# Gates of a decoder step projected feature by token from tokens scaled in place, instead of projected by token and turned

## The chip, the cores and the metric

One Trainium2 chip, one core of it. The metric is the device time of one execution in microseconds (us). All data are 32-bit floats. The engines are called by their names in the profile: PE (TensorE matmul), PEld (its weight load), DVE (VectorE), ACT (ScalarE), POOL (GpSimd) and SP (SyncE, which here only starts transfers).

## The reference, cut to what matters

The step serves 512 prompt tokens and 8 sampled ones. Each token is normed, projected by one wide matrix, attended in two head groups, gated with SiLU and projected back:

```python
def project(x, pos, lp):
    h = rms_norm(x, lp['norm_w'])
    q_n, kv_c, kv_s, kv_w, g_n, z_n, q_d, k_d, v_d, z_d = split_proj(h @ lp['w_in'])
    ...

def layer_output(x, o_branches, g_n, z_n, o_d, z_d, lam_init, lp):
    o_nsa = jnp.sum(o_branches * g_n[..., None], axis=2).reshape(B, T, NSA_WIDTH)
    o_d = (rms_norm(o_d, lp['diff_out_norm']) * (1.0 - lam_init)).reshape(B, T, DIFF_WIDTH)
    o = jnp.concatenate([o_nsa * jax.nn.silu(z_n), o_d * jax.nn.silu(z_d)], axis=-1)
    return x + o @ lp['w_out']
```

`rms_norm` multiplies a token by its inverse root mean square and by a weight for each feature. `z_n` and `z_d` are the gates: 512 features each, for every token.

## The kernel before

**Projection.** The 1024x4096 projection is cut into 8 chunks of 512 columns (one of them 280 wide) and 4 tiles of 128 tokens, so tile `n` of 32 is chunk `n // 4`, tokens `128 * (n % 4)` onward. `xt` holds the tokens turned (feature on the partitions, 8 blocks `k`), already multiplied by the feature weights but not by the inverse root means. A tile is 8 matmuls (two records each in the profile) with tokens stationary and 512 columns of weights moving (`tile`, L652); the result lies token by feature in one of two banks. ACT's `keep_tile` copies it to `proj` and multiplies by the token's inverse root mean `x_rs` (one number for each partition) on the way (L1212). For tiles 20 to 27, the gates, it also writes `exp(-z)` to `z_tmp` (L1218) and DVE's `silu_z` makes `z / (1 + exp(-z))` of the two (L1696 to L1698). The 8 sampled tokens have their own matmuls in `new_projection` (L611), scaled later by DVE's `sum_new`.

**Turning.** What comes later wants most parts feature by token. PE's `turn_blocks` transposes four 128x128 blocks into a bank (L691) and ACT's `keep_turn` copies the bank back over its source (L1258). There are 28 such turns; the last eight, `z0` to `z7`, are the gates: 32 transposes and 8 copies.

**Order.** Every engine runs one list written out by hand; semaphores join them. On PE: tiles 0 to 3; then a stage over 8 cached sequences `b` with `first_layer(b)` (L630), `second_layer(b)` (L641), two tiles each, and score matmuls of the paged cache (`k_step`, L666) between them; then 16 steps `i`, each with `tile(16 + i)` and small work. The steps at the end are:

- `i == 12`: tile 28, then 32 small score matmuls (L862), which DVE masks and centres (L1794 to L1800).
- `i == 13`: tile 29, then `z0` to `z3`.
- `i == 14`: tile 30, transposes of the window probabilities (L873) and of the compressed probabilities (L878, after DVE's `c_probs`, set at L1826), then `z4`, `z5`, then 32 matmuls that turn and weigh the differential probabilities (L888, after DVE's `diff_weights`, set at L1842, and ACT's copies of L878's result, L1359).
- `i == 15`: tile 31, one small matmul (L894), then `z6`, `z7`.

After these comes the prompt attention, 64 duos `j`: PE `scores_of` (L934), DVE `mask_max` (L1862, L1863), ACT `exps` (L1382), DVE `scale`, PE `turn` (L952), with cached value steps (L905) between. Before its first `mask_max` DVE reads L894's result (L1844) and makes the gates of the sampled tokens (L1848 to L1851).

**Early part on DVE.** `a_hidden(b)` (L1589 onward) follows each `first_layer(b)`; `a_hidden(1)` and `sum_new(1)` (L1562, L1564) stand just ahead of `a_hidden(2)`.

**Transfers.** SP loads weight chunks, cache pages and, once tile 31 is done, the cached values. A chunk of weights or a set of pages is asked for when PE has finished with the buffer's last content.

Of the kernel before, what the change touches and what calls it, by code (L numbers as in the profile page):

```python
# [7 lines left out]
ALU = mybir.AluOpType  # L8
# [3 lines left out]
P = 128  # L12
# [159 lines left out]
def program(nc, src, dst):  # L172
    ctx = ExitStack()
    with ctx:
# [99 lines left out]
        win_v = xn[:, :].rearrange("p (b k n) -> p b k n", b=DEC, k=4)  # L274
        new_z_exp = sample[:, 0:2048].rearrange("p (u n) -> p u n", u=2)[:, :, 0:512]
        row_max, row_sum = att[:, 0:8].rearrange("p (s c) -> p s c", c=2), att[:, 8:16].rearrange("p (s c) -> p s c", c=2)
        c_max, neg_rs, eps_col, out_norm = att[:, 16:48], att[:, 48:52], att[:, 52:53], norm_w[:, KC:KC + 1]
        p_turned_n = xn[:, :].rearrange("p (c k n) -> p c k n", c=4, k=TILES)
        c_exp = proj[:, :, C_KVC:C_KVC + 256].rearrange("p t (g n) -> p g t n", g=2)

# [49 lines left out]
        def bc(ap, n, at):  # L330
# [11 lines left out]
        V_NONE, V_MORE = (2, 32, 37, 40, 44, 58), (13, 16, 54, 61)  # L342

        TURNS = ["qd0", "qd1", "qd2", "qd3", "kc0", "kc1", "kc2", "kc3", "kd0", "kd1", "kv0", "kv1", "kd2", "kd3",
                 "qn0", "qn1", "qn2", "qn3", "ks", "kw", "z0", "z1", "z2", "z3", "z4", "z5", "z6", "z7"]
        N_TURNS = len(TURNS)

        def turn_number(name):
# [1 line left out]

        def turn_home(name):
            at = {"qd": C_QD, "kd": C_KD, "qn": C_QN, "kv": C_KVC, "ks": C_KS, "kw": C_KW}
            col = C_ZN + P * int(name[1:]) if name[0] == "z" else at[name[:2]] + (P * int(name[2:]) if len(name) > 2 else 0)
            return proj[:, :, col:col + P]

        def width(c):

# [232 lines left out]
        def _(pe):  # L590
# [54 lines left out]
            def tile(n):  # L645

                c, t = n // TILES, n % TILES
                if t == 0:
                    pe.wait_ge(s(w_turn(c)[0]), w_turn(c)[1])
                pe.wait_ge(s("proj_kept"), n - 1)  # L650
                for k in range(KC):
                    last = mm(banks[:, 3 + n % 2, 0:width(c)], xt[:, k, P * t:P * t + P], w_ring[:, c % 2, k, 0:width(c)],  # L652
                              start=k == 0, stop=k == KC - 1)
                last.then_inc(s("proj_ready"), 1)

            def k_step(n):
# [56 lines left out]
            new_projection(1)  # L713
            tile(5)
            second_layer(1)
            for b in range(2, DEC):
                at = K_TURN * (b - 2)
                first_layer(b)
                for n in range(at, at + 2):
                    k_step(n)  # L720
                if b < DEC - 1:
                    if b in (3, 5):
                        new_projection(b // 2 + 1)
                    tile(2 * b + 2)
                    for n in range(at + 2, at + 4):
                        k_step(n)
                    second_layer(b)
                    tile(2 * b + 3)
                else:
                    for n in range(at + 2, at + 4):  # L730
                        k_step(n)
                    pe.wait_ge(s("new_normed"), 2)
                    pe.wait_ge(s("new_proj_used"), 4)
                    cols = [C_QN + P * r for r in range(GRP)] + [C_KD + P * j for j in range(4)] + [C_KS, C_KW]
                    for n, c in enumerate(cols):
                        last = tr(banks[:, 5, 8 * n:8 * n + 8], sample[:, c:c + P], ident[0:DEC, 0:DEC])
                    last.then_inc(s("new_turned"), 1)
                for n in range(at + 4, at + k_turns(b)):
                    k_step(n)


            for i in range(16):
# [114 lines left out]
                if i == 12:  # L857
# [5 lines left out]
                                          proj[64 * g:64 * g + 64, t, C_QN + P * r:C_QN + P * r + P], p_kc_t[64 * g:64 * g + 64, :],  # L863
                                          start=True, stop=True, tile_position=(64 * g, 0))
                    last.then_inc(s("c_scored"), 1)
                if i == 13:
                    pe.wait_ge(s("z_done"), TILES)
                    for k in range(4):
                        turn_blocks(f"z{k}")
                if i == 14:  # L870
                    pe.wait_ge(s("win_vector"), step("win_probs"))
                    for kt in range(4):
                        last = tr(banks[:, 2, 64 * kt:64 * kt + 64], p_win[:, P * kt:P * kt + P], ident[0:64, 0:64])  # L873
                    last.then_inc(s("win_tensor"), 1)
                    pe.wait_ge(s("c_probs"), 1)
                    for g in range(2):
                        for t in range(TILES):
                            last = tr(banks[:, 6 + g, P * t:P * t + P], c_exp[:, g, t, :], ident)  # L878
                    last.then_inc(s("c_turned"), 1)
                    pe.wait_ge(s("z_done"), 2 * TILES)  # L880
                    turn_blocks("z4")
                    turn_blocks("z5")
                    pe.wait_ge(s("diff_weights"), 1)
                    pe.wait_ge(s("c_turned_kept"), 2)
                    for g in range(PAGES):
                        if g % 8 == 0 and g >= 16:
                            pe.wait_ge(s("probs_kept"), g // 8 - 1)
                        last = mm(banks[:, 6 + (g // 8) % 2, 64 * (g % 8):64 * (g % 8) + 64], scores[:, P * g:P * g + P], d_weights,  # L888
                                  start=True, stop=True)
                        if g % 8 == 7:  # L890
                            last.then_inc(s("probs_turned"), 1)
                if i == 15:
                    pe.wait_ge(s("new_proj_used"), 8)
                    mm(banks[0:DEC, 5, 0:DH], own_rows, own_weights, start=True, stop=True).then_inc(s("own_weighted"), 1)  # L894
                    turn_blocks("z6")
                    turn_blocks("z7")

            def v_step(v):

# [294 lines left out]
        def _(act):  # L1194
# [10 lines left out]
            def keep_tile(n):  # L1205

                c, t = n // TILES, n % TILES
                act.wait_ge(s("proj_ready"), n + 1)
                if n == 12:
                    act.wait_ge(s("normed"), 2)  # L1210
                of = banks[:, FIRST_BANKS[t] if c == 0 else 3 + n % 2, 0:width(c)]
                last = A(proj[:, t, c * CHUNK:c * CHUNK + width(c)], of, ACT.Copy, scale=x_rs[:, t:t + 1])  # L1212
                if 20 <= n < 28:
                    if n == 20:
                        act.wait_ge(s("head_means"), 4)
                    if n >= 22:
                        act.wait_ge(s("z_done"), n - 21)
                    last = A(z_tmp[:, n % 2, :], of, ACT.Exp, scale=neg_rs[:, t:t + 1])  # L1218
                last.then_inc(s("proj_kept"), 1)

            def sigmoids(b):
# [75 lines left out]
            for i in range(16):  # L1297
# [47 lines left out]
                if i == 12:  # L1345
# [4 lines left out]
                    A(scores, scores, ACT.Exp, bias=work[:, 144:145], accum_out=work[:, 145:146]).then_inc(s("diff_exps"), 1)  # L1350
                    act.wait_ge(s("c_centred"), 1)
                    A(c_exp, banks[:, 6:8, :].rearrange("p g (t n) -> p g t n", t=TILES), ACT.Exp).then_inc(s("c_exps"), 1)
                if i == 13:
                    for k in range(4):
                        keep_turn(f"z{k}")
                if i == 14:
                    act.wait_ge(s("c_turned"), 1)
                    for g in range(2):
                        A(proj[:, :, C_KVC + P * g:C_KVC + P * g + P], banks[:, 6 + g, :].rearrange("p (t n) -> p t n", t=TILES),  # L1359
                          ACT.Copy).then_inc(s("c_turned_kept"), 1)  # L1360
                    keep_turn("z4")
                    keep_turn("z5")
                    for h in range(4):
                        act.wait_ge(s("probs_turned"), h + 1)
                        A(probs_t[:, 8 * h:8 * h + 8, :].rearrange("p g n -> p (g n)"), banks[:, 6 + h % 2, :], ACT.Copy).then_inc(s("probs_kept"), 1)
                    act.wait_ge(s("new_proj_used"), 7)
                    A(new_gates, new_gates, ACT.Exp, scale=-1.0)
                    A(new_z_exp, sample[:, C_ZN:C_ZN + 1024].rearrange("p (u n) -> p u n", u=2), ACT.Exp, scale=-1.0).then_inc(s("new_z_exps"), 1)
                if i == 15:
                    keep_turn("z6")  # L1370
                    keep_turn("z7")
            act.wait_ge(s("proj_ready"), 32)
            act.wait_ge(s("new_proj_ready"), NCHUNK)

# [90 lines left out]
        def _(dve):  # L1465
# [82 lines left out]
            V.tensor_scalar(x_rs[:, :], x_rs[:, :], 1.0 / D_MODEL, EPS, ALU.mult, ALU.add).then_inc(s("x_means"), 1)  # L1548
            dve.wait_ge(s("x_roots"), 1)
            L(V.reciprocal(x_rs[:, :], x_rs[:, :]))  # L1550
            V.tensor_scalar(neg_rs, x_rs[:, 0:TILES], -1.0, None, ALU.mult).then_inc(s("x_rs_ready"), 1)

            dve.wait_ge(s("w1_in"), 48)
            L(V.tensor_tensor(pos_w1.rearrange("p k h l e -> p (k h l) e"), w1.rearrange("p k h l e -> p (k h l) e"),
# [61 lines left out]
            last.then_inc(s("q_placed"), 1)  # L1616
            a_hidden(1)
            sum_new(1)
            a_hidden(2)
            means_of(0, early_tmp)  # L1620
            a_hidden(3)
# [68 lines left out]

            def silu_z(n):

                c, t = n // TILES, n % TILES
                e, z = z_tmp[:, n % 2, :], proj[:, t, c * CHUNK:(c + 1) * CHUNK]
                dve.wait_ge(s("proj_kept"), n + 1)
                L(V.tensor_scalar(e, e, 1.0, None, ALU.add))  # L1696
                L(V.reciprocal(e, e))  # L1697
                V.tensor_tensor(z, z, e, ALU.mult).then_inc(s("z_done"), 1)  # L1698

            dve.wait_ge(s("cmp_tensor"), step("cmp_scored"))  # L1700
            V.tensor_reduce(small[0:64, 62:63], banks[0:64, 2, 0:NCMP], AX.X, ALU.max, negate=True).then_inc(s("cmp_vector"), 1)
# [464 lines left out]
```

## Time and profile before

| what | us |
|---|---|
| median of 3 executions | 790.75 |
| lowest, highest | 786.97, 792.52 |
| the profiled execution, first to last instruction | 792.1 |
| PE busy in it | 735.8 |
| DVE busy in it | 438.4 |
| ACT busy in it | 206.8 |

PE is busy in 93% of the span and leads the chain of work that ended last. Its busy time includes matmuls that overlap, so it tells how full the engine's list is and not how near the array is to its limit. Times below are microseconds from the first instruction of the profiled execution.

### The profile page before, as it was taken

How to read it: one execution, taken by the hardware profiler on the slowest of the kernel's cores; microseconds unless marked ns; L12 is line 12 of the kernel's file. 1: busy time of each engine (PE TensorE's matmuls, PEld its weight loads, DVE VectorE, ACT ScalarE, POOL GpSimd, SP SyncE). 2: the span in 40 equal slices, each digit the busy share in tenths (PEclk: the TensorE clock that was granted, in tenths of full speed). 3: DMA queues.
4: the chain of work that ended last, by engine and by line, in shares of the span. 5: the costliest groups of instructions: out<-in, count | busy, mean ns of one | idle time of the engine just before them, and what ended most of it. 6: DMA issues, size and time to landing. Idle time of an engine off the chain costs nothing.

```text
span 792.1 us, 14734 instructions
## 1 busy us (share of the span) xinstructions
PE 735.8 (93%) x4779; PEld 356.7 (45%) x4779; DVE 438.4 (55%) x945; ACT 206.8 (26%) x524; POOL 82.9 (10%) x155
## 2 busy tenths in 40 slices
PE   7999999999999999998999996898897887999997
PEld 3465645453545456443544562334443452433542
DVE  3351250805704357997563838957768656645273
ACT  0411011102010213122233323534455334333200
POOL 0000000000000000020002016500746200000000
PEclk9999999999999999998999997999999976999999
DMA  8997987999898989979788129988899939984621
GB/s 327 306 319 214 339 279 253 298 353 351 296 371 282 378 314 365 373 262 390 254 282 279 37 92 305 334 304 275 250 317 318 296 131 387 364 280 142 262 112 55
DMA packets 134552, 220.72 MB, mean 279 GB/s; under 512 B 17642, under 2 KB 58771, under 8 KB 133259
## 3 DMA queue, kind: packets, MB, share of 16 engines
q1 hardware_dynamic: 113754, 194.75, 71.7%
q0 software_dynamic: 6080, 13.25, 5.0%
q10 hardware_dynamic: 14640, 11.77, 4.8%
q8 instruction: 38, 0.62, 0.3%
q14 instruction: 40, 0.32, 0.1%
HBM read 213.84 MB, written 10.04 MB: 283 GB/s over the span
## 4 chain that ended last, share of the span: by engine, by line
PE 57%; DVE 17%; SPq 10%; DMA 8%; issue 4%; ACT 2%; POOL 0%; ACTq 0%; DVEq 0%
PE banks L652 13%; PE banks L630 13%; SPq L428 8%; PE banks L905 4%; PE banks L1036 4%; PE banks L666 4%; DMA proj<-in_cmp_cache 3%; PE banks L1157 3%; DVE att L1863 3%; DMA ring<-in_dv_cache 3%; PE banks L934 2%; PE banks L976 2%; PE banks L952 2%; DVE banks L1862 1%; PE banks L969 1%
## 5 line engine op out<-in xcount | busy, mean ns | idle before, releaser
L652 PE MATMUL banks<-ring,xt 128*128 128x512 f32 (+1 forms) x448 | 188.4, 574 | 0.0
L652 PEld LDWEIGHTS banks<-ring,xt 128*128 128x128 f32 x448 | 83.8, 192 | 93.8 <-issue 91.1
L630 PE MATMUL banks<-proj,wide 128*64 128x256 f32 x896 | 99.9, 384 | 2.2 <-DMA proj<-in_cmp_cache 2.1
L1382 ACT ACTIVATE wide<-banks,att 128x384 f32<-128x384 f32 (+3 forms) x128 | 66.4, 524 | 133.4 <-DVE att L1863 132.2
L630 PEld LDWEIGHTS banks<-proj,wide 128*64 128x64 f32 x896 | 66.3, 139 | 38.2 <-DMA proj<-in_cmp_cache 5.8
L905 PE MATMUL banks<-ring,small 128*32 128x512 f32 x512 | 71.6, 640 | 4.9 <-DMA ring<-in_dv_cache 3.3
L1589 DVE TENSOR_SCALAR small<-small 128x510 f32<-128x510 f32 x8 | 3.4, 427 | 122.8 <-ACT small L1227 106.3
L1212 ACT ACTIVATE proj<-banks,x_rs 128x512 f32<-128x512 f32 (+1 forms) x32 | 21.2, 664 | 177.0 <-PE banks L652 142.1
L666 PE MATMUL banks<-ring,small 128*32 128x512 f32 x512 | 61.4, 598 | 2.1 <-DMA ring<-in_dk_cache 2.0
L934 PE MATMUL banks<-proj 64*128 64x384 f32 (+7 forms) x256 | 54.7, 505 | 6.9 <-ACT wide L1382 6.9
L446 POOL DMA_DIRECT2D ring<-in_sel_cache x104 | 55.4, 533 | 32.9 <-issue 28.9
L1862 DVE TENSOR_TENSOR banks<-banks,consts 128x256 f32<-128x256 f32 x64 | 27.4, 428 | 55.6 <-PE banks L934 55.1
L1863 DVE TENSOR_REDUCE att<-banks 128x2 f32<-128x768 f32 (+3 forms) x64 | 52.8, 825 | 2.2
L952 PE MATMUL banks<-consts,wide 128*128 128x128 f32 x240 | 41.9, 297 | 11.9 <-DVE xt L1887 4.8
L952 PEld LDWEIGHTS banks<-consts,wide 128*128 128x128 f32 x240 | 27.7, 148 | 44.1 <-issue 18.0
L934 PEld LDWEIGHTS banks<-proj 32*128 32x128 f32 (+1 forms) x256 | 20.4, 195 | 53.6 <-issue 39.4
L598 PE MATMUL banks<-ring,xt 128*128 128x512 f32 x64 | 30.3, 638 | 5.8 <-DVE xt L1545 5.8
L1227 ACT ACTIVATE small<-banks,bias 128x255 f32<-128x255 f32 x16 | 6.7, 470 | 101.4 <-PE banks L630 88.0
L666 PEld LDWEIGHTS banks<-ring,small 128*32 128x32 f32 x512 | 13.4, 109 | 41.8 <-issue 34.9
L1157 PE MATMUL banks<-ring,proj 128*128 128x512 f32 x64 | 30.5, 630 | 0.0
L1036 PE MATMUL banks<-ring,proj 128*128 128x512 f32 x64 | 30.4, 610 | 0.0
L1697 DVE RECIPROCAL small<-small 128x512 f32<-128x512 f32 x8 | 26.8, 3353 | 0.3
(360 smaller groups left out, 829.9 us busy)
## 6 DMA issues: line engine op xcount, KB each, us to landing
ring<-in_dk_cache SPq DMA_DIRECT2D x256, 256.0 KB, 5.7
ring<-in_dv_cache SPq DMA_DIRECT2D x256, 256.0 KB, 5.5
proj<-in_cmp_cache SPq DMA_DIRECT2D x144, 128.0 KB, 3.9
ring<-in_w_in SPq DMA_DIRECT2D x6, 2048.0 KB, 12.1
proj<-in_cmp_cache ACTq DMA_DIRECT2D x80, 128.0 KB, 5.4
ring<-in_x_nat SPq DMA_DIRECT2D x2, 2048.0 KB
ring<-in_cmp_cache SPq DMA_DIRECT2D x32, 128.0 KB, 4.2
ring<-in_w_out SPq DMA_DIRECT2D x2, 2048.0 KB, 11.9
```

The costliest lines, as they stand in the source:

```text
L428: eng.dma_start(to(g), rows).then_inc(done, 16)
L446: eng.dma_start(sel_kv[64 * (n % 2):64 * (n % 2) + 64, q % 8, n // 2, :], src["sel_cache"][bass.ds(at, 1), :, :].rearrange("o k n -> (o k) ...
L630: last = mm(to, w1[:, kv, half, lp, :], rows[:, kv, g, lp, :, :, :], start=lp + half == 0, stop=lp == LP - 1 and half == 1, tile_position= ...
L652: last = mm(banks[:, 3 + n % 2, 0:width(c)], xt[:, k, P * t:P * t + P], w_ring[:, c % 2, k, 0:width(c)], start=k == 0, stop=k == KC - 1)
L666: last = mm(banks[32 * j:32 * j + 32, 6 + i % 2, :], q_blk[:, j, b, :], k_ring[:, n % 4, :, P * j:P * j + P], start=b == 0, stop=b == DEC - 1,
L905: last = mm(banks[32 * i:32 * i + 32, 7, :], probs_t[:, 4 * st + i, 32 * (b // 4):32 * (b // 4) + 32], k_ring[:, st % 4, i, :], start=st = ...
L934: last = mm(banks[:, 2 * (j % 2) + c, 0:n].rearrange("p (k n) -> p k n", n=P), proj[at:at + rows, t, q:q + P], proj[at:at + rows, 0:t + 1, ...
L952: last = tr(banks[:, 4 + (kind if kind < 2 else c), P * k:P * k + P], e_slot(j, c)[:, P * k:P * k + P], ident)
L1036: last = mm(banks[:, 6, :], out_block(t, k), w_out[:, k, 512 * c:512 * c + 512], start=k == 0, stop=k == KC - 1)
L1157: last = mm(banks[:, 2 * t + c, :], out_block(t, k), w_out[:, k, 512 * c:512 * c + 512], start=k == 0, stop=k == KC - 1)
L1382: last = A(e_slot(j, c)[:, 0:n], banks[:, 2 * (j % 2) + c, 0:n], ACT.Exp, bias=row_max[:, j % 4, c:c + 1], accum_out=row_sum[:, j % 4, c:c ...
L1863: V.tensor_reduce(row_max[:, j % 4, :], both[:, :, 0:n], AX.X, ALU.max, negate=True).then_inc(s("maxed"), 1)
```

## The change

Two sets of edits belong together. First, the prompt tokens in `xt` are multiplied by their inverse root means. For this PE spreads `x_rs` over the partitions (four matmuls of 128x128, with a column of `x_rs` broadcast as the stationary side and the identity moving, into bank 7), placed after `second_layer(1)`; DVE then multiplies `xt` in place by that bank, placed after `sum_new(1)`. DVE waits for tiles up to 5 (they still use the unscaled tokens), and tile 6 waits for DVE. From tile 6 on ACT copies with a scale of 1.

Second, the gate tiles 20 to 27 exchange the operands: a block of 128 weight columns is stationary and all 512 tokens move, so that a tile is 128 features by 512 tokens and goes straight to its place in `z_t`. The turns `z0` to `z7` and their copies go, and with them two waits of PE for `z_done`.

```diff
         TURNS = ["qd0", "qd1", "qd2", "qd3", "kc0", "kc1", "kc2", "kc3", "kd0", "kd1", "kv0", "kv1", "kd2", "kd3",
-                 "qn0", "qn1", "qn2", "qn3", "ks", "kw", "z0", "z1", "z2", "z3", "z4", "z5", "z6", "z7"]
+                 "qn0", "qn1", "qn2", "qn3", "ks", "kw"]
...
+        Z_TILES = range(20, 28)
+        X_NORMED = 6
+
+        def tile_home(n):
+
+            c, t = n // TILES, n % TILES
+            if n in Z_TILES:
+                return z_t(n - Z_TILES[0])
+            return proj[:, t, c * CHUNK:c * CHUNK + width(c)]
...
                 pe.wait_ge(s("proj_kept"), n - 1)
+                if n == X_NORMED:
+                    pe.wait_ge(s("x_normed"), 1)
                 for k in range(KC):
-                    last = mm(banks[:, 3 + n % 2, 0:width(c)], xt[:, k, P * t:P * t + P], w_ring[:, c % 2, k, 0:width(c)],
-                              start=k == 0, stop=k == KC - 1)
+                    if n in Z_TILES:
+                        of, by = w_ring[:, c % 2, k, P * t:P * t + P], xt[:, k, 0:SEQ]
+                    else:
+                        of, by = xt[:, k, P * t:P * t + P], w_ring[:, c % 2, k, 0:width(c)]
+                    last = mm(banks[:, 3 + n % 2, 0:width(c)], of, by, start=k == 0, stop=k == KC - 1)
...
             tile(5)
             second_layer(1)
+            for t in range(TILES):
+                last = mm(banks[:, 7, P * t:P * t + P], x_rs[:, t:t + 1].broadcast_to([P, P]), ident, start=True, stop=True)
+            last.then_inc(s("rs_spread"), 1)
...
-                if i == 13:
-                    pe.wait_ge(s("z_done"), TILES)
-                    for k in range(4):
-                        turn_blocks(f"z{k}")
...
-                    pe.wait_ge(s("z_done"), 2 * TILES)
-                    turn_blocks("z4")
-                    turn_blocks("z5")
                     pe.wait_ge(s("diff_weights"), 1)
                     pe.wait_ge(s("c_turned_kept"), 2)
...
-                    turn_blocks("z6")
-                    turn_blocks("z7")
...
-                last = A(proj[:, t, c * CHUNK:c * CHUNK + width(c)], of, ACT.Copy, scale=x_rs[:, t:t + 1])
-                if 20 <= n < 28:
+                to = tile_home(n)
+                if n in Z_TILES:
+                    of = of.rearrange("p (t n) -> p t n", t=TILES)
+                last = A(to, of, ACT.Copy, scale=x_rs[:, t:t + 1] if n < X_NORMED else 1.0)
+                if n in Z_TILES:
...
-                    last = A(z_tmp[:, n % 2, :], of, ACT.Exp, scale=neg_rs[:, t:t + 1])
+                    last = A(z_tmp[:, n % 2, :].rearrange("p (t n) -> p t n", t=TILES), of, ACT.Exp, scale=-1.0)
...
             a_hidden(1)
             sum_new(1)
+            dve.wait_ge(s("rs_spread"), 1)
+            dve.wait_ge(s("proj_ready"), X_NORMED)
+            x_prompt = xt[:, :, 0:SEQ]
+            V.tensor_tensor(x_prompt, x_prompt, bc(banks[:, 7, :], KC, 1), ALU.mult).then_inc(s("x_normed"), 1)
             a_hidden(2)
```

## Rows read from the trace of the kernel before

**Rows 1.** The page's head: span and instructions.

```profile
span 792.1 us, 14734 instructions
```

**Rows 2.** The chain that ended last, as shares of the span by engine.

```profile
PE 57%; DVE 17%; SPq 10%; DMA 8%; issue 4%; ACT 2%; POOL 0%; ACTq 0%; DVEq 0%
```

**Rows 3.** Windows: stretch, length, busy of each engine (records), granted clock, DMA, GB/s.

```profile
434.00:443.00 9.00, 9.00 (x23) 4.05 (x22) 8.83 (x9) 2.61 (x4) 2.04 (x5) 0.81 0.14 37
...
476.00:484.00 8.00, 2.33 (x14) 0.66 (x12) 7.30 (x13) 1.25 (x5) 5.63 (x11) 0.67 1.04 306
```

**Rows 4.** Timeline of PE, 430 to 483: start, length, line, tiles, records [idle before].

```profile
429.98 3.76 PE L862 MATMUL banks<-picked,proj 64*128 64x32 f32 x64
433.67 8.83 PE L652 MATMUL banks<-ring,xt 128*128 128x512 f32 x16
442.34 1.04 PE L691 MATMUL banks<-consts,proj 128*128 128x128 f32 x8
443.77 1.15 PE L691 MATMUL banks<-consts,proj 128*128 128x128 f32 x8 [0.39 <-ACT proj L1258]
444.75 7.03 PE L652 MATMUL banks<-ring,xt 128*128 128x512 f32 x16
451.71 0.46 PE L873 MATMUL banks<-consts,small 64*128 64x64 f32 x4
452.11 1.09 PE L878 MATMUL banks<-consts,proj 128*128 128x128 f32 x8
...
454.46 7.33 PE L888 MATMUL banks<-work,wide 128*128 128x64 f32 x64 [0.39 <-ACT proj L1359]
461.63 7.08 PE L652 MATMUL banks<-ring,xt 128*128 128x512 f32 x16
...
482.82 1.65 PE L934 MATMUL banks<-proj 64*128 64x384 f32 x4 [5.67 <-ACT wide L1382]
```

**Rows 5.** Timeline of DVE over the same stretch.

```profile
433.79 1.30 DVE L1794 TENSOR_TENSOR banks<-banks,consts 128x512 f32<-128x512 f32 x2 [7.88 <-PE banks L862]
...
450.11 1.29 DVE L1826 TENSOR_TENSOR proj<-proj,att 128x512 f32<-128x512 f32 x2
452.21 0.42 DVE L1830 COPY spread<-banks 128x256 f32<-128x256 f32 x1 [0.81 <-PE banks L873]
...
453.98 0.25 DVE L1842 TENSOR_SCALAR work<-consts,small 128x64 f32<-128x64 f32 x1
468.88 0.15 DVE L1844 COPY small<-banks 8x8 f32<-8x8 f32 x1 [14.66 <-PE banks L894]
...
480.46 0.96 DVE L1863 TENSOR_REDUCE att<-banks 128x2 f32<-128x768 f32 x1
```

**Rows 6.** Timeline of ACT: the copies that L888 waits for.

```profile
453.24 1.08 ACT L1359 ACTIVATE proj<-banks 128x512 f32<-128x512 f32 x2 [0.73 <-PE banks L878]
```

**Rows 7.** Timeline of PE and DVE, 82 to 102.

```profile
82.51 2.31 DVE L1564 SCALAR_TENSOR_TENSOR sample<-banks,x_rs,sample 8x512 f32<-8x512 f32 x3
85.74 1.05 PE L641 MATMUL banks<-w,small 128*128 128x128 f32 x8
86.72 14.03 PE L630 MATMUL banks<-proj,wide 128*64 128x256 f32 x128
...
101.72 0.43 DVE L1589 TENSOR_SCALAR small<-small 128x510 f32<-128x510 f32 x1 [16.90 <-ACT small L1227]
```

**Rows 8.** Groups by line and form: busy, mean ns of one, idle before.

```profile
L1036 PE MATMUL banks<-ring,proj 128*128 128x512 f32 x64 | 30.4, 610 | 0.0
...
L1672 DVE TENSOR_TENSOR xn<-xn,kc_stats 128x2048 f32<-128x2048 f32 x1 | 2.3, 2293 | 0.0
```

**Rows 9.** PE at 122, and windows of PE alone: stretch, length, busy (records), clock, DMA, GB/s.

```profile
122.02 1.06 PE L666 MATMUL banks<-ring,small 128*32 128x512 f32 x8 [1.54 <-DMA ring<-in_dk_cache]
...
124.00:128.00 4.00, 4.00 (x26) 0.61 1.06 389
434.00:438.00 4.00, 4.00 (x6) 0.57 0.17 42
```

More of the change, by code:

```diff
@@ L276, in program @@
         row_max, row_sum = att[:, 0:8].rearrange("p (s c) -> p s c", c=2), att[:, 8:16].rearrange("p (s c) -> p s c", c=2)
-        c_max, neg_rs, eps_col, out_norm = att[:, 16:48], att[:, 48:52], att[:, 52:53], norm_w[:, KC:KC + 1]
+        c_max, eps_col, out_norm = att[:, 16:48], att[:, 52:53], norm_w[:, KC:KC + 1]
         p_turned_n = xn[:, :].rearrange("p (c k n) -> p c k n", c=4, k=TILES)
@@ L352, in turn_home @@
             at = {"qd": C_QD, "kd": C_KD, "qn": C_QN, "kv": C_KVC, "ks": C_KS, "kw": C_KW}
-            col = C_ZN + P * int(name[1:]) if name[0] == "z" else at[name[:2]] + (P * int(name[2:]) if len(name) > 2 else 0)
+            col = at[name[:2]] + (P * int(name[2:]) if len(name) > 2 else 0)
             return proj[:, :, col:col + P]
+        Z_TILES = range(20, 28)
[5 more added lines that the diff above has]
+            return proj[:, t, c * CHUNK:c * CHUNK + width(c)]
         def width(c):
@@ L1352, in _ @@
                     A(c_exp, banks[:, 6:8, :].rearrange("p g (t n) -> p g t n", t=TILES), ACT.Exp).then_inc(s("c_exps"), 1)
-                if i == 13:
-                    for k in range(4):
-                        keep_turn(f"z{k}")
                 if i == 14:
@@ L1360, in _ @@
                           ACT.Copy).then_inc(s("c_turned_kept"), 1)
-                    keep_turn("z4")
-                    keep_turn("z5")
                     for h in range(4):
@@ L1368, in _ @@
                     A(new_z_exp, sample[:, C_ZN:C_ZN + 1024].rearrange("p (u n) -> p u n", u=2), ACT.Exp, scale=-1.0).then_inc(s("new_z_exps"), 1)
-                if i == 15:
-                    keep_turn("z6")
-                    keep_turn("z7")
             act.wait_ge(s("proj_ready"), 32)
@@ L1550, in _ @@
             L(V.reciprocal(x_rs[:, :], x_rs[:, :]))
-            V.tensor_scalar(neg_rs, x_rs[:, 0:TILES], -1.0, None, ALU.mult).then_inc(s("x_rs_ready"), 1)
+            dve.sem_inc(s("x_rs_ready"), 1)
             dve.wait_ge(s("w1_in"), 48)
@@ L1691, in silu_z @@
             def silu_z(n):
-                c, t = n // TILES, n % TILES
-                e, z = z_tmp[:, n % 2, :], proj[:, t, c * CHUNK:(c + 1) * CHUNK]
+                e, z = z_tmp[:, n % 2, :], tile_home(n)
                 dve.wait_ge(s("proj_kept"), n + 1)
@@ L1697, in silu_z @@
                 L(V.reciprocal(e, e))
-                V.tensor_tensor(z, z, e, ALU.mult).then_inc(s("z_done"), 1)
+                V.tensor_tensor(z, z, e.rearrange("p (t n) -> p t n", t=TILES), ALU.mult).then_inc(s("z_done"), 1)
             dve.wait_ge(s("cmp_tensor"), step("cmp_scored"))
```

## Prediction

> **What bounds the kernel now.** I began with the page's head and the chain of work that ended last. The profiled execution spans 792.1 us [rows 1]; the runs' median is 790.75, 0.2% less. I work with differences and add them to the median. PE holds 57% of the chain and DVE 17% [rows 2], so one cannot say for the whole kernel that a microsecond of PE work is a microsecond of time. Each stage has to be read by itself.
>
> The removed work stands at one place, the last three steps before the prompt attention, so next I read the windows there and then the timelines of PE, DVE and ACT side by side. From 434 to 443 PE is full (9.00 of 9.00) but its granted clock is 0.81 on the mean, and DVE is full as well (8.83) [rows 3]. From 476 to 484 PE works 2.33 of 8 us while DVE works 7.30: the attention's first scores lie ready, and DVE still has the sampled tokens' gates to make [rows 3, 5]. PE sits idle 5.67 us there [rows 4]. The reader is to see that two engines take turns at the end of this stage: PE to L862, then DVE and PE side by side, then PE through L888 and tile 31, then DVE alone from 468.88 to the first maxima at 481.4 [rows 4, 5].
>
> **What is removed, and what it is worth.** On PE 32 transposes go, in four pairs of turns. The first two pairs fill the time from tile 29's last matmul (442.34) to tile 30's first (444.75): 2.41 us with a wait of 0.39 for ACT in it [rows 4]. The third pair stands between L878 (which begins at 452.11 and takes 1.09) and L888, about 1 us. The fourth, again about 1 us, stands behind tile 31 and L894. Counted as PE time this is 2.4 + 1.0 + 1.0, some 4.4 us, and with the wait ahead of L888 (0.39) 4.8. I now go through what each is worth on the path.
>
> The first two pairs: without them tile 30 starts at 442.34 and, at 7.03 less the overlap of its start, is through at about 449.4. L873 follows to about 449.8. L878 then waits for DVE's `c_probs`. DVE's list from 433.79 to the end of L1826 at 451.40 has no wait on anything of PE behind L862, and the change takes nothing from it [rows 5]. So L878 starts at about 451.5 and not at 452.11: of 2.4 us, 0.6 us come through, and the rest turns into a wait of PE of some 1.6 us.
>
> The third pair: behind L878 (1.05 us, to 452.55) ACT copies two banks, 1.08 us from 453.24 in the trace, so from 452.6 to 453.7 after the change [rows 6]. L888 waits for this copy before and after; z4 and z5 lay in its shadow. Adding the same 0.13 from ACT's end to PE's start (454.32 to 454.46), L888 begins at 453.8 in place of 454.46. DVE's other release, the end of L1842, was at 454.23 because DVE had waited 0.81 us for L873 [rows 5]; it moves to 453.4 and is not last. The first three pairs together are worth 454.46 - 453.83 = 0.63 us. What was queued behind them on ACT (copies of `probs_turned`) follows L888's matmuls and moves with them.
>
> The fourth pair is off the path. L894 stands before it, DVE takes over at L894's end, and PE's next needed product waits for DVE until 482.82. One microsecond less only makes the idle 5.67 some 1 us longer. The 8 ACT copies lie in ACT's idle time and are worth nothing by themselves. If DVE's list were no longer the cover (the rival below), the whole 4.8 us would count.
>
> **What is added.** (a) The spread: four 128x128 matmuls. These are matmuls and not transposes. The nearest row is `second_layer`: 4 matmuls of the same shape show as 8 records in 1.05 us (0.98 to the next start) [rows 7]. I take +1.0 us. It stands in front of `first_layer(2)`, whose end releases the next page loads, and PE goes on with no gap there. The lower bound is 0.4: SP's loads may absorb part of it, since PE waits for pages (1.54 us at 120.5) soon after [rows 9]. The upper is 1.1.
>
> (b) The scaling in place on DVE, 4096 elements a partition. The nearest row is 2048 elements of two operands in 2.29 us [rows 8], so 4.6 us. It can start when the spread is done, about 87.8. DVE has been idle since 84.8 and has nothing until 101.72, because `a_hidden(2)` waits for `first_layer(2)` [rows 7]. It ends at about 92.5. Tile 6, behind `first_layer(2)` (to 100.7) and two score steps, waits for it but finds it done 9 us before. Cost 0. Were the 14.03 us of `first_layer(2)` not there, the 4.6 would stand open on PE.
>
> (c) The exchanged operands. A gate tile remains 8 matmuls of 128x512 with a 128x128 weight load. The trace has such matmuls with other sources: L1036, ring moving and `proj` stationary, 610 ns a record [rows 8]. In full runs they start about 0.45 us apart against 0.44 (7.03 / 16) in a tile. I take 0; if the gate tiles took that pace, 128 records by 0.013 are +1.7. A gain is excluded, since number, width and weight columns are equal. DVE and ACT keep their elements; the stored pieces only lie apart. No transfer is added or moved, and POOL's list is untouched.
>
> Sum on the path: +1.0 - 0.6 = +0.4 us.
>
> **The clock.** Then there is what the new gap does. PE will have only 0.45 us of L873 and 1.05 us of L878 between 449.4 and 453.8, and then 7.33 us of L888, on which everything waits. The trace shows what follows such stretches. After 1.54 us idle, 1.06 us of narrow matmuls and another 0.42 idle at 120.5 to 123.5, the window from 124 has a granted clock of 0.61, most of it the lower of the two levels, 1.2 GHz in place of 2.4 [rows 9]. After L862's 3.76 us of small matmuls the clock is 0.57 from 434 to 438, and tile 29 takes 8.83 us in place of 7.03 to 7.08: 1.8 us lost [rows 4, 9]. I take it that the clock falls once in the new gap and price it by tile 29's loss, +1.7 us. The bounds are 0 (it does not fall) and about +3 (L878 falls into it too, and the low level goes on into L888). If tile 29 is spared instead, nothing is won: PE only waits longer for DVE.
>
> The Trainium skill speaks against the change here: "TensorE: Matmul & The Clock Gate", section "HAM oscillation — how this bites in real kernels", has TensorE go back to half rate in waits between bursts of matmuls and the next burst start slow. By that rule it would be +2.1 us, without it +0.4. The half-speed stretches above agree; that none follows 451.7 to 454.5 in this trace, where transposes fill the time, speaks neither way.
>
> So +0.4 + 1.7 = +2.1 us, and 790.75 + 2.1 = 792.9.
>
> **Rivals.**
>
> 1. *The clock holds in the gap.* Only the sum counts: 791.2. For it speaks that L878 and L873 break the gap in two. Against it is that the windows above fell after less.
>
> 2. *All the removed PE time comes through.* It needs DVE not to be the bound between 433.8 and 451.4. Then -4.8 + 1.0 = -3.8, so 787.0. Against it stands that DVE is busy with hardly a gap over that stretch.
>
> 3. *Slower.* Weights from the ring as the stationary side and `xt` as the moving one pace the 8 gate tiles worse than any row shows. Each tile lies on PE's path. It decides (over 1% slower, 7.9 us) once a tile takes (7.9 - 2.1) / 8 = 0.7 us more than 7.03. The nearest row gives a fifth of a microsecond, 794.6. At 0.8 us a tile it would be 799.3.
>
> 4. *The scaling is exposed* (its cover is thinner than read): up to 4.6 more, 797.5. It needs DVE to begin 9 us late.
>
> **How the numbers follow.** Forecast 0.50, rival 1 0.32, rival 2 0.06, rival 3 0.08 (of it 0.04 over 1%), rival 4 0.02, the remainder 0.02 anywhere. The runs of before lie from 787.0 to 792.5, so a median is uncertain by about 2 us by itself. The range takes rival 1 with 3 us below (788.0) and the forecast with its upper clock bound and the slower pace (792.9 + 1.3 + 1.7, about 796.0). About 1% is what a measurement of this kernel can tell from no change: faster 0.03, within 1% 0.92, slower 0.05.
>
> **What the profile after would show.** 8 records of a 128x128 matmul ahead of the third `first_layer`, about 1 us. A DVE multiplication of 4.6 us within its idle time and no wait of PE for it. L652 on the gate tiles at 574 to 610 ns. No turn between tiles 29 and 30; a wait of PE on DVE of about 1.6 us ahead of L878, and one on ACT of 1.2 us ahead of L888. A granted clock near 0.5 in a part of L888. An idle of 6 to 7 us before the first scores are used. The prediction is wrong if L878 starts with tile 30's end (DVE had room), if L888 begins less than 19 us after the end of L862 (20.7 before, 20.1 forecast), or if a gate tile takes more than 7.3 us at full clock.

## The result and the profile after

The changed kernel takes 796.61 us on the median of 20 executions (788.39 to 802.77), the kernel before 790.51 (786.2 to 794.97, also 20). The ratio is 1.0068, with a 95% interval of 1.0042 to 1.0093: slower by some 5.4 us, where 2.1 were forecast. It lies within 1%. The ratios here and below leave out executions more than 1.5% above the fastest of the same kernel (here 801.57 and 802.77), so they need not match the medians, which are 6.1 us apart here. The changed kernel's executions fall apart into two groups: three at 788.4, 788.7 and 789.7, and seventeen from 793.9 up.

The page's head and its chain of work, of the changed kernel:

```profile
span 795.9 us, 14679 instructions
...
PE 57%; DVE 19%; SPq 10%; DMA 8%; issue 4%; ACT 2%; POOL 0%; ACTq 0%; DVEq 0%
```

The profiled executions differ by 3.8 us (792.1 before, [rows 1]). As shares the chain has hardly changed [rows 2], so the page doesn't tell where the 3.8 us lie. The timeline of PE around the removed turns does (line numbers of the changed kernel: L880 is the former L862, L887 L873, L892 L878, L899 L888, L668 the tiles):

```profile
425.64 3.76 PE L880 MATMUL banks<-picked,proj 64*128 64x32 f32 x64
429.33 15.70 PE L668 MATMUL banks<-ring,xt 128*128 128x512 f32 x32
444.96 0.46 PE L887 MATMUL banks<-consts,small 64*128 64x64 f32 x4
447.12 1.09 PE L892 MATMUL banks<-consts,proj 128*128 128x128 f32 x8 [1.70 <-DVE proj L1833]
449.47 13.19 PE L899 MATMUL banks<-work,wide 128*128 128x64 f32 x64 [1.27 <-ACT proj L1368]
462.46 9.50 PE L668 MATMUL banks<-ring,xt 128*128 128x512 f32 x16
...
486.06 1.65 PE L943 MATMUL banks<-proj 64*128 64x384 f32 x4 [6.80 <-ACT wide L1386]
```

L899 are the 32 matmuls that turn and weigh the differential probabilities; they are called the weighing matmuls below. Compare with [rows 4]. From the small score matmuls to the weighing matmuls (L862 to L888 before, L880 to L899 after) it is 24.48 us before and 23.83 after: 0.65 less, as forecast. Then the weighing matmuls take 13.19 us where they took 7.33 (+5.9), and tile 31 takes 9.50 where it took 7.08 (+2.4). The windows tell why. Columns as in [rows 3], the granted clock being the last but two:

```profile
445.00:449.00 4.00, 1.51 (x13) 1.13 (x12) 3.66 (x16) 1.35 (x3) 0.00 (x0) 1.00 0.12 33
450.00:462.00 12.00, 12.00 (x59) 12.00 (x59) 0.00 (x0) 1.79 (x3) 0.00 (x0) 0.51 0.13 36
462.00:467.00 5.00, 5.00 (x10) 2.42 (x10) 0.00 (x0) 1.65 (x3) 0.00 (x0) 0.50 0.14 40
467.00:472.00 5.00, 5.00 (x18) 2.00 (x20) 0.00 (x0) 0.01 (x1) 0.00 (x0) 0.97 0.06 17
```

In the gap PE works 1.51 of 4 us. Behind it the granted clock goes to 1.2 GHz, 0.8 us after L899 has begun (at 450.2), and stays there for 17 us, through the rest of L899 and the first half of tile 31. PE is 100% busy in that time; by its busy share nothing is to be seen.

The difference of the two profiled executions, cut at the same marks:

| stretch | before | after | difference |
|---|---|---|---|
| start to the small score matmuls | 430.0 | 425.6 | -4.4 |
| from there to the weighing matmuls | 24.5 | 23.8 | -0.7 |
| weighing matmuls and tile 31, to the small matmul behind (L894, after L905) | 14.2 | 22.4 | +8.2 |
| from there to the first scores behind the wait | 14.2 | 14.2 | 0.0 |
| from there to the first value matmuls (L969, after L978) | 30.6 | 32.5 | +1.9 |
| from there to PE's end | 272.9 | 271.6 | -1.3 |

The first row is no gain of the change; it even holds the added spread. The place where the small score matmuls start moves from profile to profile: 425.6 and 431.1 in two other kernels with the gates turned as before (`before_move31_early` and `scale_only` below). In the profile of before the clock is low at 124 to 128 [rows 9] and again from 366 to 372 (the `new_projection` at 368.15 takes 3.60 us there, 1.90 in the changed kernel's profile), and the waits for cache pages differ by a microsecond or two. Such stretches differ from execution to execution. The +1.9 at the start of the attention is of this sort too: the clock is low for 17 us there after and for 10 before. With the scaling alone, where the turns are all in place, that stretch also takes 32.6 us, and with both gaps of the changed kernel filled (`fill_dense` below) 30.3. So one profile of each kernel shows 3.8 where the medians show 6.1.

The two added pieces, on PE and DVE in the changed kernel:

```profile
86.93 1.05 PE L651 MATMUL banks<-w,small 128*128 128x128 f32 x8
87.82 1.06 PE L732 MATMUL banks<-consts,x_rs 128*128 128x128 f32 x8
88.80 14.03 PE L640 MATMUL banks<-proj,wide 128*64 128x256 f32 x128
...
88.91 4.42 DVE L1626 TENSOR_TENSOR xt<-xt,banks 128x4096 f32<-128x4096 f32 x1 [2.90 <-PE banks L732]
...
103.81 0.43 DVE L1593 TENSOR_SCALAR small<-small 128x510 f32<-128x510 f32 x1 [10.47 <-ACT small L1239]
```

The spread takes 0.98 us to the next start. The scaling takes 4.42 us of time in which DVE was idle before [rows 7], with 10.47 us idle left behind it. PE has no wait for it.

### The profile page after: what moved, and what is told of

It reads as the page before. It is cut to its first block, busy times and chain, and to the rows that moved or that the text cites. A ratio compares the mean times of both kernels' runs of the same rounds, so it can differ in the third digit from the quotient of the medians.

```text
span 795.9 us, 14679 instructions
## 1 busy us (share of the span) xinstructions
PE 738.1 (93%) x4755; PEld 359.5 (45%) x4755; DVE 442.7 (56%) x945; ACT 199.4 (25%) x516; POOL 82.2 (10%) x155
## 4 chain that ended last, share of the span: by engine, by line
PE 57%; DVE 19%; SPq 10%; DMA 8%; issue 4%; ACT 2%; POOL 0%; ACTq 0%; DVEq 0%
PE banks L640 14%; PE banks L668 12%; SPq L438 7%; PE banks L914 4%; PE banks L1045 4%; DMA proj<-in_cmp_cache 4%; PE banks L681 4%; PE banks L1166 3%; DVE att L1870 3%; DMA ring<-in_dv_cache 2%; PE banks L943 2%; PE banks L985 2%; PE banks L899 2%; PE banks L961 2%; DVE banks L1869 1%
## 5 line engine op out<-in xcount | busy, mean ns | idle before, releaser
L668 PE MATMUL banks<-ring,xt 128*128 128x512 f32 (+1 forms) x320 | 133.4, 571 | 0.0
L668 PEld LDWEIGHTS banks<-ring,xt 128*128 128x128 f32 x320 | 60.8, 195 | 66.1 <-issue 63.4
L914 PE MATMUL banks<-ring,small 128*32 128x512 f32 x512 | 73.6, 657 | 4.3 <-DMA ring<-in_dv_cache 2.7
L943 PE MATMUL banks<-proj 64*128 64x384 f32 (+7 forms) x256 | 56.5, 520 | 8.0 <-ACT wide L1386 8.0
L681 PE MATMUL banks<-ring,small 128*32 128x512 f32 x512 | 61.1, 598 | 1.6 <-DMA ring<-in_dk_cache 1.6
L668 PE MATMUL banks<-xt,ring 128*128 128x512 f32 x128 | 56.7, 595 | 0.0
L1224 ACT ACTIVATE proj<-banks 128x512 f32<-128x512 f32 (+1 forms) x26 | 14.8, 568 | 157.5 <-PE banks L668 136.1
L668 PEld LDWEIGHTS banks<-xt,ring 128*128 128x128 f32 x128 | 23.7, 190 | 28.6 <-issue 28.5
L1045 PE MATMUL banks<-ring,proj 128*128 128x512 f32 x64 | 30.4, 610 | 0.0
```

The costliest lines, as they stand in the source:

```text
L668: last = mm(banks[:, 3 + n % 2, 0:width(c)], of, by, start=k == 0, stop=k == KC - 1)
L681: last = mm(banks[32 * j:32 * j + 32, 6 + i % 2, :], q_blk[:, j, b, :], k_ring[:, n % 4, :, P * j:P * j + P], start=b == 0, stop=b == DEC - 1,
L914: last = mm(banks[32 * i:32 * i + 32, 7, :], probs_t[:, 4 * st + i, 32 * (b // 4):32 * (b // 4) + 32], k_ring[:, st % 4, i, :], start=st = ...
L943: last = mm(banks[:, 2 * (j % 2) + c, 0:n].rearrange("p (k n) -> p k n", n=P), proj[at:at + rows, t, q:q + P], proj[at:at + rows, 0:t + 1, ...
L1045: last = mm(banks[:, 6, :], out_block(t, k), w_out[:, k, 512 * c:512 * c + 512], start=k == 0, stop=k == KC - 1)
```

## The experiments

The theory after the result: the turns `z4` and `z5`, in ACT's shadow as they were, kept PE at work between L878 and L888. Without them the clock falls there, and the 64-column matmuls behind don't raise it again. Rivals: the exchanged operands or the scaled tokens cost the time, or it is lost elsewhere. The first gap is PE's wait for DVE ahead of L892 (1.70 us in the profile above), the second its wait for ACT ahead of L899 (1.27 us). In the edits `mm` is a matmul and `tr` a transpose on PE; what they write to `banks[:, 0]` nobody reads. All ratios are to the kernel before on the same chip, whose median was 789.99 us (`fill_dense`, `fill_turns`, `scale_only`, `no_turns`), 790.35 (`lift`, `move31`, `move31_early`, `before_move31_early`) or 789.86 (the rest).

**Both gaps filled with dense matmuls.**

```diff
                     last.then_inc(s("win_tensor"), 1)
+                    pe.wait_ge(s("turned_kept"), N_TURNS)
+                    for f in range(2):
+                        mm(banks[:, 0, :], xt[:, f, 0:P], xt[:, f, 0:SEQ], start=True, stop=True)
                     pe.wait_ge(s("c_probs"), 1)
...
                     last.then_inc(s("c_turned"), 1)
+                    for f in range(1):
+                        mm(banks[:, 0, :], xt[:, f, 0:P], xt[:, f, 0:SEQ], start=True, stop=True)
                     pe.wait_ge(s("diff_weights"), 1)
```

> The changed kernel with three extra 128x512 matmuls of no use on PE, two in the wait ahead of L892 (1.7 us in the changed kernel's profile) and one in the wait for ACT ahead of L899 (1.3 us); nothing else differs and their result goes to an idle bank. Theory 'clock': the changed kernel loses its time because the gap left by the turns lets the clock fall and the 64-column matmuls of L899 don't raise it again. Then L899 takes 7.3 us (13.2 in the changed kernel), tile 31 7.1 (9.5), and the time is that of before plus 1.0 less 0.6: ratio about 0.998 to 1.003. Rival 'operands or place': L899 and tile 31 are slow for another reason (where the gates now lie, the scaled tokens), or the loss is elsewhere: L899 stays near 13 us and the ratio near 1.007.

Measured: 789.6, ratio 0.9978 (0.9945 to 1.0012). Timeline of PE, and a window with the granted clock last but two:

```profile
453.80 7.33 PE L904 MATMUL banks<-work,wide 128*128 128x64 f32 x64 [0.41 <-ACT proj L1373]
460.97 7.08 PE L668 MATMUL banks<-ring,xt 128*128 128x512 f32 x16
...
454.00:461.00 7.00, 7.00 (x65) 1.00 0.16 44
```

Three matmuls whose result nobody reads win the time back (by the medians 789.6 against 789.99). Both lengths are those of before [rows 4], and the clock holds. The operands, the scaling and the place of the gates are as in the changed kernel, so none of them is the cause by itself.

**Both gaps filled with transposes.** The same edit with `tr(banks[:, 0, ...], proj[:, f % 4, C_QD:C_QD + P], ident)`, 12 in the first gap and 8 in the second.

> The changed kernel with 12 transposes of 128x128 in the first gap and 8 in the second (the work that the removed turns did, without ACT's copies and on other data, result unused). Theory 'clock, transposes count': they hold the clock as the removed turns seem to have done; L899 7.3 us, ratio about 1.000. Rival 'transposes don't count': the clock falls all the same, L899 near 13 us in most executions, ratio about 1.007; then the kernel before kept its clock for another reason (the shorter gap).

Measured: 790.28, ratio 0.9994 (0.9971 to 1.0017), L904 again 7.33 us. Transposes do here for the clock what dense matmuls do, as the removed turns did.

**One gap filled.** The 12 transposes in the first gap alone, and the 8 in the second alone.

> The changed kernel with 12 transposes of no use in the first gap alone (ahead of L892, where PE waits for DVE); the 1.3 us wait for ACT ahead of L899 stays empty. Theory 'the gap next to L899 is enough' (move31, which has that gap alone, lost time): the clock falls in L899 in more than half of the executions, ratio 1.003 to 1.006. Rival 'the long first gap is the cause and the second harmless': ratio about 1.000, as with both filled.

> The changed kernel with 8 transposes of no use in the second gap alone (between L892 and L899); PE still idles 1.7 us for DVE ahead of L892. Theory 'the gap next to L899 decides': ratio 1.000 to 1.003, L899 at 7.3 us in most executions. Rival 'the first gap decides': ratio near 1.006 and L899 near 13 us.

Measured: first gap filled 794.84, ratio 1.0092 (1.0056 to 1.0127), more than the 1.003 to 1.006 expected; second gap filled 790.65, ratio 1.0022 (0.9994 to 1.0049), as expected. So the 1.27 us ahead of L899 are enough to lose the time, and the wait for DVE that I had counted as the larger gap costs little by itself. That it costs nothing is not shown: with the second gap filled five of twelve executions still lie together at 793.4 to 794.4, and the one profile of that kernel (788.7) had only 0.64 us of idle time in the first gap. The profiled execution with only the first gap filled was itself one of the short ones (788.8):

```profile
448.94 1.09 PE L895 MATMUL banks<-consts,proj 128*128 128x128 f32 x8 [0.27 <-DVE proj L1836]
451.30 7.33 PE L902 MATMUL banks<-work,wide 128*128 128x64 f32 x64 [1.27 <-ACT proj L1371]
```

The same gap of 1.27 us and no fall: the clock doesn't fall in every execution. Below 791 us lay one of that kernel's six executions, three of the changed kernel's twenty and six of twelve with the second gap filled, against sixteen of 23 of the kernel before beside these last.

**The scaling alone.** The kernel before with the spread, the scaling in place and scale 1 on ACT; gates turned as before.

```diff
             second_layer(1)
+            for t in range(TILES):
+                last = mm(banks[:, 7, P * t:P * t + P], x_rs[:, t:t + 1].broadcast_to([P, P]), ident, start=True, stop=True)
+            last.then_inc(s("rs_spread"), 1)
```

> The kernel before with the scaling of the tokens alone (spread matmuls, DVE's multiplication in place, ACT copies with scale 1); gates token by feature and turned as before. Theory: only the spread's 1.0 us counts, ratio 1.001 (+1 us), clock low stretches as in before. Rival 'the scaling carries the loss': ratio near 1.007.

Measured: 790.56, ratio 1.0005 (0.9974 to 1.0035). One microsecond fits; 5 don't.

**The turns left out, nothing put in their place.** The kernel before without the eight gate turns, their copies and PE's two waits.

```diff
-                if i == 13:
-                    pe.wait_ge(s("z_done"), TILES)
-                    for k in range(4):
-                        turn_blocks(f"z{k}")
...
-                    turn_blocks("z4")
-                    turn_blocks("z5")
```

> The kernel before with the eight gate turns and their copies left out and nothing put in their place (the gates are read in the wrong layout, so this part of the computation is left out). Theory 'clock': the gap opens here too, L888 takes some 13 us in most executions, and the kernel is slower than before though it does less: ratio about 1.005 to 1.007 (before - 0.6 us + some 6 us in most executions). Rival 'the exchanged operands or the scaling carry the loss': ratio 0.999 or below, down to 0.994 if all 4.8 us come through.

Measured: 799.37, ratio 1.0135 (1.0099 to 1.0171), all six executions above 797. A kernel that only does less is 1.35% slower. Timeline of PE, and windows across the weighing matmuls and tile 31:

```profile
448.71 1.09 PE L874 MATMUL banks<-consts,proj 128*128 128x128 f32 x8 [0.62 <-DVE proj L1809]
451.07 11.57 PE L881 MATMUL banks<-work,wide 128*128 128x64 f32 x64 [1.27 <-ACT proj L1347]
462.43 9.49 PE L652 MATMUL banks<-ring,xt 128*128 128x512 f32 x16
...
454.00:462.00 8.00, 8.00 (x39) 0.50 0.13 35
462.00:467.00 5.00, 5.00 (x9) 0.50 0.12 33
```

The scaled tokens and the exchange are both absent here, and the loss is there all the same. In this profile the first gap is only 0.62 us and the clock falls nevertheless. The ratio is double what I expected, and more than the changed kernel's. These two lengths account for 6.6 us of it (20.8 in place of 14.2, start to start), and the start of the attention has 1.9 more, as in the changed kernel's profile; where the rest lies is not traced.

**The exchange alone.** The changed kernel without the scaling (the gates are then not multiplied by the inverse root means).

> The changed kernel without the scaling of the tokens: gates feature by token with weights stationary, but not multiplied by the inverse root means (this part of the computation is left out), no spread matmuls, the other tiles scaled by ACT as before. Theory: the time of the changed kernel less the spread's 1.0 us: ratio 1.005 to 1.006. With no_turns (1.0135, gates token by feature) as the neighbour, the difference between the two is the operand exchange by itself: rival 'the exchange makes gate tiles faster' if this is 3 us or more below no_turns.

Measured: 797.83, ratio 1.0119 (1.0084 to 1.0153), its weighing matmuls 11.40 us. The expected 1.005 to 1.006 was too low. Next to the turns left out (1.0135) the exchange by itself makes no difference that can be told. Both lose more than the changed kernel (1.0068, interval up to 1.0093); by the medians it is 9.4 and 8.0 us against 6.1. The clock doesn't fall in every execution, and six executions each don't settle whether the scaling has a part in how often it does; this stays open.

**Dense matmuls inside the weighing matmuls.** Four 128x512 matmuls after the first 8 of L899's 32, gaps left open.

```diff
+                        if g == 8:
+                            pe.wait_ge(s("turned_kept"), N_TURNS)
+                            for f in range(4):
+                                mm(banks[:, 0, :], xt[:, f, 0:P], xt[:, f, 0:SEQ], start=True, stop=True)
```

> The changed kernel with four extra 128x512 matmuls of no use after the first 8 of the 32 matmuls of L899 (result to an idle bank); the gaps stay as they are. Theory: the clock falls in the gap, and the 64-column matmuls don't raise it again while dense 128x512 ones do. Then the first 8 run slow (about 0.41 us each, as 13.2 / 32 in the changed kernel), the clock rises within the extra matmuls or just behind them, the other 24 take 5.5 us (0.23 each) and tile 31 takes 7.1 instead of 9.5. Rival 'the low stretch has its own length or goes on for another reason': the clock stays low through the rest of L899 and into tile 31 as before.

Measured in a single execution: the clock didn't fall there at all.

```profile
453.46 1.97 PE L903 MATMUL banks<-work,wide 128*128 128x64 f32 x16 [1.27 <-ACT proj L1372]
455.27 3.65 PE L900 MATMUL banks<-xt 128*128 128x512 f32 x8
458.76 5.47 PE L903 MATMUL banks<-work,wide 128*128 128x64 f32 x48
```

All three run at full pace, so there was nothing to lift, and this run tells nothing of what raises the clock (798.55 us in that one execution, of which the extra matmuls are 3.5). That 64-column matmuls don't raise it is therefore read from the profiles in which it fell, and no run has tested it.

**Tile 31 moved into the first gap.**

```diff
-                tile(16 + i)
+                if i < 15:
+                    tile(16 + i)
...
                     last.then_inc(s("win_tensor"), 1)
+                    tile(31)
                     pe.wait_ge(s("c_probs"), 1)
```

> The changed kernel with tile 31 moved on PE into the wait for the compressed probabilities (behind L887, ahead of L892), where 1.7 us lay idle. Theory: PE has dense work where the gap was, the clock holds, and tile 31's first 1.7 us are free: first L914 about 2.3 us earlier than in before's profile, plus the spread's 1.0: ratio 0.997 to 0.999, no stretch of half clock in L899. Rival 'the 1.3 us wait for ACT is enough to let it fall': L899 near 13 us, ratio 1.005 or more.

Measured: 793.74, ratio 1.0034 (1.0005 to 1.0063). The ratio lies between the theory (up to 0.999) and the rival (1.005 or more); the profile is the rival's. The first gap is gone, yet the clock falls, 2.4 us after the weighing matmuls have begun:

```profile
457.98 1.04 PE L894 MATMUL banks<-consts,proj 128*128 128x128 f32 x8
460.29 11.73 PE L901 MATMUL banks<-work,wide 128*128 128x64 f32 x64 [1.27 <-ACT proj L1370]
472.71 3.64 PE L916 MATMUL banks<-ring,small 128*32 128x512 f32 x16 [0.55 <-ACT small L1374]
```

**The sampled gates made early as well.** As the last one, with the small matmul L905 ahead of L899 and ACT's exponentials for the sampled gates ahead of its copies; then the same two moves on the kernel before; then the first of them with 8 transposes in the second gap.

```diff
                     pe.wait_ge(s("diff_weights"), 1)
+                    pe.wait_ge(s("new_proj_used"), 8)
+                    mm(banks[0:DEC, 5, 0:DH], own_rows, own_weights, start=True, stop=True).then_inc(s("own_weighted"), 1)
                     pe.wait_ge(s("c_turned_kept"), 2)
```

> As move31, and the small matmul L905 goes ahead of L899, with ACT's exponentials of the sampled tokens' gates ahead of its copies, so that DVE makes the sampled gates (9.5 us) while PE works in L899 and not behind it. Theory: the 6.8 us in which PE waits for the first exponentials shrink to 1 or 2, and the removed turns count in full because PE now bounds this stage: 7 us less than before, ratio about 0.991. Rival 'the cached values or the attention loop take it back': less than 3 us.

> The kernel before (gates turned) with the same two moves as move31_early. Theory: PE bounds this stage here too, so now the turns cost what they take on PE: about 5 us less than before (0.994), 2.4 us more than move31_early (4 us of turns less 1.0 of the spread and what is hidden). Rival 'the change is worth nothing even here': equal to move31_early within 1 us.

> move31_early with 8 transposes of no use in the wait for ACT ahead of the weighing matmuls, the one gap that it has left there. Theory: what move31_early still loses to the clock in some executions goes, ratio 0.993 to 0.996 (move31_early 0.9964). Rival: its clock was held already and what bounds it now is the supply of cached values, so that the ratio stays at 0.996.

| kernel | median us | ratio | 95% interval |
|---|---|---|---|
| changed, both moves | 787.45 | 0.9964 | 0.9939 to 0.9988 |
| before, both moves | 787.24 | 0.9972 | 0.9943 to 1.0002 |
| changed, both moves, 8 transposes | 788.86 | 0.9988 | 0.9965 to 1.0012 |

All three win less than expected; in each the rival came out (less than 3 us won, the two kernels equal, nothing from the transposes). In the first kernel the wait ahead of the first used scores shrinks as foreseen, to 1.09 us, and they start at 475.4 in its profile, 7.4 earlier than in [rows 4]. The first value matmuls then start only 3.3 us earlier than before (510.1 against 513.4). The waits of PE between 474 and 512, in that kernel:

```profile
PE banks L917 <- DMA ring<-in_dv_cache: 4.3, 4, 2.5
PE banks L946 <- ACT wide L1389: 2.6, 2, 1.5
```

and between 481 and 515 in the kernel before:

```profile
PE banks L934 <- ACT wide L1382: 6.5, 2, 5.7
PE banks L905 <- DMA ring<-in_dv_cache: 1.3, 3, 0.5
```

The wait for the exponentials has become in part a wait for cached values: 3.0 us more of it, while the transfer engines are full in both stretches (busy share 1.01 and 1.07). The two kernels with both moves are equal, so in this order too the removed turns are worth nothing that can be measured; what takes back the 3 to 4 us of their PE time is not shown. The transposes added to it win nothing.

## Why the prediction was right or wrong

**The bound of the stage: right.** DVE's list ends `c_probs` at 447.05, PE waits 1.70 us for it (1.6 forecast) and 1.27 for ACT (1.2), and the weighing matmuls start 20.1 us after the small score matmuls' end (20.1 forecast, 20.7 before). Of 4.8 us of removed PE time 0.65 came through. The fourth pair only lengthened the idle time, from 5.67 to 6.80.

**The added work: right.** +0.98 for the spread (1.0 forecast), none for the scaling (4.42 us, 4.6 forecast), none for the exchange. The gate tiles take 7.03 to 7.13 us at full clock; a record's mean is 595 ns, against 602 before:

```profile
L668 PE MATMUL banks<-xt,ring 128*128 128x512 f32 x128 | 56.7, 595 | 0.0
```

**The clock: right in kind, wrong in size.** The step that failed is "I take it that the clock falls once in the new gap and price it by tile 29's loss, +1.7 us", with its upper bound of about +3. The profile of the changed kernel shows +5.9 on the weighing matmuls and +2.4 on tile 31, 8.3 in all. The row was of the wrong kind. Tile 29 is made of 128x512 matmuls, and the low stretch in it lasted 3.4 us (434.3 to 437.7). Even that row was one of several: with the turns left out the low stretch there lasts 6.8 us (429.7 to 436.5). Behind the new gap stand 64-column matmuls, and in all four profiles in which the clock fell there (the changed kernel, the turns left out, the exchange alone, tile 31 moved) it stayed low to their end, through 8.7 to 12.4 us of them. The whole low stretch was 17 us here and 13.6 with the turns left out. It came back 4.8 to 5.2 us into tile 31, or, where that had been moved away, in the value matmuls behind. So not the fall alone is the price, but the fall times the work that stands behind it. The three of twenty executions that lie at 788.4 to 789.7 fit a clock that held, and then the change is as good as free.

It is partly luck that the result lies at the end of the recorded range and not far beyond it. The ratio on the medians of before (790.5 and 790.75) gives 795.9 to 796.1 us, where the range ended at about 796.0. But 1.7 of that was for gate tiles of a slower pace, which didn't come. With the clock's upper bound alone the range would have ended at 794.2.

**Which gap: partly wrong.** I treated the 4.4 us between tile 30 and L888 as one gap. The fillings show that its last 1.27 us, ahead of the weighing matmuls, are enough, and that the first 1.7 by themselves cost at most 0.5% (1.0022, interval up to 1.0049).

**The chances.** The clock case had 0.50 and "the clock holds" 0.32; measured, 17 of 20 executions look like the first by their times and mean clocks (only one of them has a trace). The row that spoke for it was weighed too low: at 123.5 [rows 9] the clock fell after 1.54 and 0.42 us of idle time, less than the new gap has. The other stretch of [rows 9] follows 3.76 us of small matmuls with no idle time, so it is no row for a lull. That the clock held behind 451.7 to 454.5 in the kernel before, the prediction says, "speaks neither way". This was a misreading: `z4` and `z5` were at work there, and filling that place again with transposes of no use brought the time back. The Trainium skill's rule, "TensorE: Matmul & The Clock Gate", section "HAM oscillation — how this bites in real kernels", has waits between bursts of matmuls make the next burst start slow. The trace agrees in kind; the waits in the page's example are longer than the 1.27 us that were enough here.

**The slower rivals** (pace of the gate tiles, exposed scaling) are excluded by the rows above, and "all the removed PE time comes through" by the 1.70 us that PE waits for DVE.

## What to carry to other kernels

Work that lies in another engine's shadow can still pay for itself: ask of every PE instruction you take out what PE does in its place, and whether what stands behind the hole can bring the clock back. Price a fall of the clock by the work that follows it (its full length again for the small matmuls here), not by the last fall that you find in the trace. Before a stage's PE work is cut, read which engine ends its waits; if that is another one, cut there or move dense work into the hole.

## What the runs showed of the hardware

- The clock fell behind a lull of about a microsecond: 1.27 us idle after 1.04 us of transposes, in front of small matmuls, with dense work ahead of both (`move31`). It doesn't fall every time: the same lull left the clock at 2.4 GHz in the profiled executions with the first gap filled and of `lift`. Of the changed kernel's twenty executions the three short ones have a mean granted clock of 0.965 to 0.971, the others 0.947 to 0.962; of 81 executions of the kernel before, in the runs beside the experiments, one has 0.962 and the rest 0.963 or more (its profiled execution, of 792.5 us, has 0.962 too).
- 64 records of 128x64 matmuls, back to back and 100% busy, ran at 1.2 GHz from the fall to their end (13.19 us in place of 7.33), while in tiles of 128x512 behind them the full clock came back, after 4.8 us here. At 2.4 GHz the same 64 records kept it when the hole ahead of them was filled.
- Transposes held the clock in such a hole. The Trainium skill, "TensorE: Matmul & The Clock Gate", section "Part 4: PE-mode transpose", says that transposes don't count as busy TensorE in the way matmuls do; 20 transposes in the two holes gave 0.9994 here, three dense matmuls 0.9978, with intervals that overlap, and the weighing matmuls took 7.33 us with either. So here they did hold it, against the page; whether they can raise it, no run shows.
- The kernel that leaves out 32 transposes and 8 copies and puts nothing in their place was 1.35% slower (1.2% by the medians).
